# A two-layer decoder trunk on one core: the residual gates summed and spread by one product with ones, their bias by a transfer, and the adaLN vectors in another order

## The reference, cut to what matters

```python
c_act = jax.nn.silu(c)
for l in range(DEPTH):
    mod = (c_act @ w_ada[l] + b_ada[l])[:, None, :]
    sh1, sc1, gt1, sh2, sc2, gt2 = jnp.split(mod, 6, axis=-1)
    h = x * (1.0 + sc1) + sh1
    y = hybrid_mixer(h, positions, w_in[l], ...)      # window attention and top-k attention
    x = layer_norm(ALPHA * x + (1.0 + gt1) * y, ...)
    h = x * (1.0 + sc2) + sh2
    y = swiglu(h, w_gate[l], w_up[l], w_down[l])      # 1024 -> 2816 -> 1024
    x = layer_norm(ALPHA * x + (1.0 + gt2) * y, ...)
```

## Time and profile before

| | before |
|---|---|
| median of three runs | 1346.01 us |
| the profiled execution's own time | 1347.72 us |
| its span, first to last instruction | 1346.0 us |
| granted TensorE clock, mean | 0.982 |
| TensorE busy | 1266.8 us, 94% |
| VectorE, ScalarE, GpSimd busy | 61%, 37%, 21% |

### The profile page before, as it was taken

How to read it: one execution, slowest core, us unless ns; L and a number is a source line. 1 busy time by engine, 2 the same in 40 slices (tenths; PEclk the granted TensorE clock), 3 DMA queues, 4 the chain that set the end, 5 groups by cost and what they waited for, 6 DMA issues and landing times.

```text
span 1346.0 us, 18459 instructions
## 1 busy us (share of the span) xinstructions
PE 1266.8 (94%) x6392; PEld 1048.8 (78%) x6392; DVE 818.3 (61%) x1444; ACT 503.8 (37%) x1013; POOL 276.7 (21%) x287
## 2 busy tenths in 40 slices
PE   2798998999999999999999999899999999999996
PEld 2585876788888877888878888778888887888885
DVE  6667899757777756433266678975743355333337
ACT  0444657615333311232225455673443331222320
POOL 1084135811111100000002546563000000000001
PEclk9798999999899999999999999999999999999998
DMA  9553112242888725222222320011332223233311
GB/s 330 202 192 124 63 48 63 84 152 65 279 272 273 257 103 188 94 93 93 78 78 94 95 78 17 1 64 44 102 106 93 93 93 125 94 95 100 101 47 63
DMA packets 44272, 156.17 MB, mean 116 GB/s; under 512 B 5808, under 2 KB 5808, under 8 KB 44208
## 3 DMA queue, kind: packets, MB, share of 16 engines
q1 hardware_dynamic: 30528, 109.07, 24.2%
q0 software_dynamic: 12672, 46.14, 10.3%
q10 hardware_dynamic: 1008, 0.12, 0.1%
HBM read 153.21 MB, written 2.10 MB: 115 GB/s over the span
## 4 chain that ended last, share of the span: by engine, by line
PE 73%; DVE 13%; issue 4%; ACT 3%; POOL 3%; DMA 3%; SPq 0%; DVEq 0%; ACTq 0%; POOLq 0%
PE bank L539 22%; PE bank L541 21%; PE bank L540 21%; PE bank L805 2%; PE bank L772 2%; DMA ada_w<-in_w_ada 2%; DVE scores L1438 2%; DVE w_lo L1310 2%; DVE top L1430 2%; PE bank L751 2%; DVE ada_acc L1333 1%; DMA w_raw<-in_weights 1%; PE bank L783 1%; DVE xs L1540 1%; DVE pq L1477 1%
## 5 line engine op out<-in xcount | busy, mean ns | idle before, releaser
L539 PE MATMUL bank<-hT_hi,w_hi 128*128 128x512 f32 (+1 forms) x768 | 287.2, 374 | 2.2 <-issue 1.5
L540 PE MATMUL bank<-hT_lo,w_hi 128*128 128x512 f32 (+1 forms) x768 | 285.8, 372 | 0.0
L541 PE MATMUL bank<-hT_hi,w_lo 128*128 128x512 f32 (+1 forms) x768 | 285.7, 372 | 0.0
L1696 DVE TENSOR_TENSOR w_lo<-w_raw,w_hi 128x1024 fp32r<-128x1024 f32 x88 | 107.8, 1225 | 146.3 <-ACT w_hi L1220 146.3
L539 PE MATMUL bank<-w_hi,hT_hi 128*128 128x512 f32 (+2 forms) x448 | 172.1, 384 | 10.8 <-DVE hT_lo L1395 7.1
L1064 ACT ACTIVATE w_hi<-w_raw 128x1024 fp32r<-128x1024 f32 x96 | 100.5, 1061 | 211.5 <-PE bank L541 208.4
L539 PEld LDWEIGHTS bank<-hT_hi,w_hi 128*128 128x128 f32 x768 | 145.1, 189 | 28.1 <-issue 2.2
L541 PE MATMUL bank<-w_hi,hT_lo 128*128 128x512 f32 (+2 forms) x448 | 165.5, 369 | 0.0
L540 PE MATMUL bank<-w_lo,hT_hi 128*128 128x512 f32 (+2 forms) x448 | 165.3, 369 | 0.0
L541 PEld LDWEIGHTS bank<-hT_hi,w_lo 128*128 128x128 f32 x768 | 145.0, 189 | 25.3
L540 PEld LDWEIGHTS bank<-hT_lo,w_hi 128*128 128x128 f32 x768 | 145.1, 189 | 25.1
(11 more groups left out here) (144 smaller groups left out, 1894.9 us busy)
## 6 DMA issues: line engine op xcount, KB each, us to landing
w_raw<-in_weights SPq DMA_DIRECT2D x184, 512.0 KB, 3.4
ada_w<-in_w_ada POOLq DMA_DIRECT2D x80, 512.0 KB, 5.1
ada_w<-in_w_ada SPq DMA_DIRECT2D x16, 512.0 KB, 5.1
xs<-in_x SPq DMA_DIRECT2D x4, 512.0 KB, 9.2
g_row<-in_ln_row POOLq DMA_DIRECT2D x4, 512.0 KB, 5.6
b_row<-in_ln_row POOLq DMA_DIRECT2D x4, 512.0 KB, 6.3
trunk_out<-xs SPq DMA_DIRECT2D x8, 256.0 KB, 2.0
modb<-in_b_ada ACTq DMA_DIRECT2D x1, 48.0 KB, 3.7
```

Of the source, the lines that this page charges most:

```text
L539: pe.matmul(dst, a_hi, b_hi, start=first, stop=False)
L540: pe.matmul(dst, a_hi, b_lo, start=False, stop=False)
L541: return pe.matmul(dst, a_lo, b_hi, start=False, stop=last)
L1696: nc.vector.tensor_tensor(w_lo[:, s, :], w_raw[:, s, :], w_hi[:, s, :].bitcast(F32), ALU.subtract).then_inc(lo_ready, 1)
```

## The change: what it does

The vectors are made in the order sh1, sc1, sh2, sc2, gt1 of layer 0, then sh1, sc1, sh2, sc2 of layer 1, then gt2 of layer 0, gt1 and gt2 of layer 1. The first four, and the four of layer 1, remain in column form; they are the only ones that are reduced. A gate's accumulator is instead multiplied by a 128 by 128 matrix of ones, which sums over the partitions and puts the sum on all of them. Its bias comes as a row to `scratch` by a broadcast transfer (GpSimd issues that of the first gate at step 33 of attention, ScalarE that of the second behind group 0's `feed`), and `take_gate` computes (sum + 1) + bias.

The accumulations keep their places up to vector 4. Turn 0 of the loop has none; turns 1 to 4 have vectors 5 to 8, turn 5 vector 9. Vector 10 is accumulated after DN00's residuals, and vector 11 after DN01's. The wait for the taken vectors moves from DN00's first tile to its last. `reduce_ada` writes to bank 3 and not to bank 0. In `build_h` the wait for `gt_spread` becomes one for `gt_taken`.

```diff
-SH1, SC1, GT1, SH2, SC2, GT2 = range(6)
+SH1, SC1, SH2, SC2, GT1, GT2 = range(6)
+ADA_ORDER = ((0, SH1), (0, SC1), (0, SH2), (0, SC2), (0, GT1), (1, SH1), (1, SC1), (1, SH2), (1, SC2),
+             (0, GT2), (1, GT1), (1, GT2))
+ADA_COLUMNS = 8
...
+        def acc_of(g):
+
+            return g % 2 if g < 5 else int(g not in (9, 11))
...
+                    if i == ROPE_AT[-1]:
+                        pool.wait_ge(roped, at_roped(l, 4, T - 1))
+                        pool.dma_start(scratch[:], b_gate[2 * l].to_broadcast([P, D_MODEL])).then_inc(gate_in[0], 16)
...
             def spread_gate(l, which, b):
 
-                pe.wait_ge(gt_diag, 2 * l + which + 1)
+                g = ADA_ORDER.index((l, (GT1, GT2)[which]))
+                pe.wait_ge(ada_used, (g + 1) * KD)
                 for half in range(2):
-                    m = pe.matmul(bank[b + half][:], ones[:], scratch[:, half * 512:(half + 1) * 512],
+                    m = pe.matmul(bank[b + half][:], ones[:], ada_acc[:, acc_of(g), half * 512:(half + 1) * 512],
...
-                    if l == 0:
-                        reduce_ada(0)
                 else:
                     pe.wait_ge(z_done, at_z(l, DN00, T - 1))
-                with pe.Fori(1 - g, FG[g] // 2) as i:
-                    for j in range(4):
-                        wait_turn(j, i)
-                        product(j, slice(0, SEQ)).then_inc(piece_used, 1)
-                    if (l, g) == (0, 0):
-                        reduce_ada(i)
+                with_ada = (l, g) == (0, 0)
+                for i0, i1 in ((1, 5), (5, 6)) if with_ada else ((1 - g, FG[g] // 2),):
+                    with pe.Fori(i0, i1) as i:
+                        for j in range(4):
+                            wait_turn(j, i)
+                            product(j, slice(0, SEQ)).then_inc(piece_used, 1)
+                        if with_ada and i1 == 5:
+                            reduce_ada(i)
...
-                        pe.wait_ge(mod_taken, 5 + FG[0] // 2)
+                    elif q == DN00 and t == T - 1:
+
+                        pe.wait_ge(mod_taken, ADA_COLUMNS)
...
                 if l == 0:
-                    reduce_mod(3, 7, KD)
-                    reduce_mod(4, 7)
+                    reduce_mod(3, 7)
...
-                    if (l, g) == (0, 1):
-
-                        reduce_mod(6 * DEPTH - 1, 7)
...
+                act.wait_ge(h_lo, at_tile(2 * l + 1, T - 1))
+                act.wait_ge(h_hi, at_tile(2 * l + 1, T - 1))
+                act.dma_start(scratch[:], b_gate[2 * l + 1].to_broadcast([P, D_MODEL])).then_inc(gate_in[1], 16)
...
             def take_gate(l, which, b):
+
+                dve.wait_ge(gate_in[which], 16 * (l + 1))
                 dve.wait_ge(gt_spread, 2 * l + which + 1)
                 for half in range(2):
-                    m = nc.vector.tensor_copy(gt_row[:, half * 512:(half + 1) * 512], bank[b + half][:])
+                    cols = slice(half * HALF, (half + 1) * HALF)
+                    m = nc.vector.scalar_tensor_tensor(out=gt_row[:, cols], in0=bank[b + half][:], scalar=1.0,
+                                                       in1=scratch[:, cols], op0=ALU.add, op1=ALU.add)
...
-                    if i == GATE_AT:
-                        gate_diagonal(l, 0)
...
+                for i0, i1 in ((0, 1), (1, 5), (5, 6)) if with_ada else ((0, FG[g] // 2),):
+                    with dve.Fori(i0, i1) as i:
+                        for f in range(2):
+                            if with_ada and i0 > 0:
+                                ada_pieces(i, ada_acc[:, acc_of(4 + i0), :], 4 * f, 4 * f + 4)
...
-                gate_diagonal(l, 1)
...
                     for t in range(T):
                         residual(l, q, t, True)
-                    if (l, half) == (0, 0):
-                        ada_group(6 * DEPTH - 1)
+                    if l == 0:
+                        ada_group(10 + half)
```

More of the change, by code:

```diff
@@ L557, in transpose_x, with reduce_mod @@
                 m.then_inc(x_transposed, 1)
[L559 removed]
+            def reduce_mod(g, b):
                 if g == 0:
@@ L564, in reduce_mod @@
                 for k in range(KD):
-                    m = pe.matmul(bank[b][:, c0 + k:c0 + k + 1], ada_acc[:, g % 2, k * P:(k + 1) * P], ones[:, 0:1],
+                    m = pe.matmul(bank[b][:, k:k + 1], ada_acc[:, g % 2, k * P:(k + 1) * P], ones[:, 0:1],
                                   start=True, stop=True)
@@ L1325, in ada_piece, with take_mod @@
                     dve.wait_ge(ada_in[n % RING], 16 * ((n - 2 * KD) // RING + 1))
+                acc = ada_acc[:, acc_of(g), :]
                 if k == 0:
[L1327 to L1331, removed]
-                else:
[L1333 to L1337, removed]
+                    if g == 11:
+                        dve.wait_ge(gt_spread, 2)
+                    elif g >= 2:
+                        dve.wait_ge(mod_reduced, min(g - 1, ADA_COLUMNS))
+                    nc.vector.tensor_scalar(acc, ada_w[:, n % RING, :], cc[:, 1, 0:1], None, ALU.mult)\
+                        .then_inc(ada_used, 1)
+                else:
+                    nc.vector.scalar_tensor_tensor(out=acc, in0=ada_w[:, n % RING, :], scalar=cc[:, 1, k:k + 1],
+                                                   in1=acc, op0=ALU.mult, op1=ALU.add).then_inc(ada_used, 1)
+            def take_mod(g, b):
                 dve.wait_ge(mod_reduced, g + 1)
-                nc.vector.tensor_tensor(mod[:, g, :], bank[b][:, c0:c0 + KD], modb[:, g, :], ALU.add)\
+                nc.vector.tensor_tensor(mod[:, g, :], bank[b][:, 0:KD], modb[:, g, :], ALU.add)\
                     .then_inc(mod_taken, 1)
@@ L1707, in ada_pieces @@
                         else:
                             dve.wait_ge(ada_used, i * KD + n)
[L1709 to L1711 removed]
+                            m = nc.vector.scalar_tensor_tensor(out=acc, in0=ada_w[:, n % RING, :],
+                                                               scalar=cc[:, 1, k:k + 1], in1=acc,
+                                                               op0=ALU.mult, op1=ALU.add)
@@ L1712, in ada_pieces @@
                         m.then_inc(ada_used, 1)
[L1714 to L1727, removed]
-                                                gu_hi[:, at, :].bitcast(F32), ALU.subtract).then_inc(gu_lo_ready, 1)
-                        dve.wait_ge(gu_lo_ready, i * 2 + (f0 + f + 1))
-                    if with_ada:
-                        dve.wait_ge(mod_reduced, i + 6)
-                        nc.vector.tensor_tensor(mod[:, bass.ds(i + 5, 1), :],
-                                                bank[0][:, 0:KD].unsqueeze(1),
-                                                modb[:, bass.ds(i + 5, 1), :], ALU.add).then_inc(mod_taken, 1)
@@ L1890 @@
     one, zero = np.ones((D_MODEL,), np.float32), np.zeros((D_MODEL,), np.float32)
+    b_vectors = b_ada.reshape(DEPTH, 6, D_MODEL)
+    order = [6 * l + (0, 1, 3, 4, 2, 5)[v] for l, v in ADA_ORDER]
     rows = np.stack([np.stack([g, b]) for l in range(DEPTH)
```

67 lines of the change are left out of this document (34 added, 33 removed).

## The result

| | before | after |
|---|---|---|
| median | 1345.87 us (6 runs, 1343.45 to 1348.15) | 1337.07 us (6 runs, 1334.94 to 1339.17) |
| ratio, 95% interval | | 0.9936 [0.9923, 0.9949] |
| profiled execution, its span | 1347.72, 1346.0 us | 1335.96, 1334.2 us |
| granted TensorE clock, mean | 0.982 | 0.989 |

The kernel became 8.8 us faster, with an interval that excludes 1; 6.3 were forecast, and the new median lies within the stated range. The page of the kernel after, engine totals and chain by engine, beside the earlier trace rows: 64 matmuls less, and TensorE's share of the chain stays the largest.

What follows compares the result with a forecast made beforehand. TensorE, busy 94% of the span, was taken as the bound. Removed work and waits of 16.5 us, less 3.4 for the spread and 6.8 for vector 11, gave -6.3: median 1346.0 to 1339.7 us, range 1334.0 to 1343.5.

Steps and rivals of the forecast that it cites:

- Reductions at 1.7 us each: Four of twelve reductions on TensorE go; those between WO0 and WO1 and ahead of DN10 save 1.7 us each.
- Turn 0, -7.8: End of group 0's turn 0: a 2.71 us wait, a 1.7 reduction and 3.4 of lower clock go, 7.8 us.
- Turn 5 to DN00, -5.3: Between turn 5 and DN00: reduction and wait of 3.7 us and 1.65 of lower clock go, 5.3 us.
- The spread, +3.4: Ahead of layer 0's first gate spread: TensorE waits 1.8 us, the clock falls for 1.65; cost 3.4 us.
- Vector 11, +6.8: Group 1's third product waits 5.1 us behind vector 11, plus 1.7 for a clock fall; cost 6.8 us.
- DN01, nothing: The stretch of DN01 in layer 0 was forecast to change by 0 us.
- (a): Rival, chance 0.14: group 1's stall only 1.7 us without a fall, none in attention; -13.0 us, 1333.
- Diagonals, takings, transfers, sums: nothing: Four diagonals and takings removed from VectorE count nothing; added bias-row transfers and sums cost nothing to under 0.1 us each.
- (b): Rival, chance 0.10: turn 1 finds low halves or raw pieces late, turn 0 gives only 1.7; -0.2 us, 1345.8.
- (c): Rival, chance 0.08: vector 11's first four pieces not loaded at 545.9, stall 12.5 us, fall 3.4; +2.8 us, 1348.8.

Runs made afterwards that it cites:

- e6_reduce5: The kernel after with one reduction more at the end of turn 5, its vector waited for at DN00's last tile: 1337.23 us, ratio 0.9938.
- e2_turn0: Against `e3_gate0`, layer 1's four columns come first, in turns 0 to 3, and are reduced there; gates follow in turns 4 and 5: 1335.59 us, ratio 0.9922.
- e3_gate0: The kernel after with layer 0's second gate as vector 5, summed in turn 0 and not reduced; nothing in DN01: 1329.87 us, ratio 0.9878.
- e4_late_spread: The kernel after with the spread of each layer's first gate behind WO0's first tile, not ahead of it: 1334.34 us, ratio 0.9910.
- e7_reduce5_wait: As `e6_reduce5`, but with the wait for the taken vector at DN00's first tile, as in the kernel before: 1341.99 us, ratio 0.9963.
- e1_swap: The kernel after with the low halves of group 1's third and fourth piece ahead of vector 11 in VectorE's queue: 1329.87 us, ratio 0.9877.
- after_again: The kernel after measured once more, with no edit: 1338.2 us, ratio 0.9933 to the kernel before.

## Why the prediction was right, term by term

- *Reductions at 1.7 us each.* Right. Measured 1.8 between WO0 and WO1, 1.8 ahead of DN10, 1.8 in `e6_reduce5`. The earlier trace rows gave it.
- *Turn 0, -7.8.* Right: -7.9, and 7.96 the other way in `e2_turn0`. That it is a wait for a result and no lack of room on VectorE was read from the earlier trace rows and argued from 5.8 us of slack in the earlier trace rows; `e3_gate0` showed it.
- *Turn 5 to DN00, -5.3.* Right, in its parts too: 1.8, 1.6 and 1.6 in the two kernels that put them back.
- *The spread, +3.4.* Here a term was mis-sized: +1.4 was measured. The idle time is 1.41, not 1.8: the last piece took 1.28 us and not the 1.66 of the earlier trace rows, as VectorE's timeline of the kernel after has it:

```profile
265.28 0.69 DVE L1530 TENSOR_TENSOR hT_lo<-bank,hT_hi 128x512 fp32r<-128x512 f32 x1
265.88 1.28 DVE L1346 SCALAR_TENSOR_TENSOR ada_acc<-ada_w,cc,ada_acc 128x1024 f32<-128x1024 f32 x1
```

And the clock did not fall behind it, in none of the seven profiles (of six kernels) that have the wait. I had taken the fall on the strength of the earlier trace rows, where waits of 1.52 and 1.85 bring it and one of 1.80 does not; between such rows it was a guess. The same trace has another wait of 1.80 us, up to 218.86, with 0.50 behind it, which I had not read (more in the last section). The sum came out within 2.5 us of the measured time in spite of this term, not by it. The term is 2.0 of the 2.6 us by which the sum fell short of the -8.9 of the trace.
- *Vector 11, +6.8.* Right: +7.1. Order 2.1 (1.7 forecast), waits for `ada_w` 3.3 in this profile (3.4 forecast from the earlier trace rows; 1.7 to 2.9 in the other four), fall of the clock 1.7. In `e4_late_spread` and `e7_reduce5_wait` the clock stayed at 0.50 for 6.8 us there, the upper bound of the forecast. `e1_swap` removed the whole by an exchange of two blocks.
- *DN01, nothing.* 0.5 us more was gained. One of its pieces had been waiting for a low half behind old vector 11, 0.25 us of idle time in the record and a start 0.4 late, and does so no more:

```profile
527.20 0.47 PE L539 MATMUL bank<-w_hi,gu_hi 128*128 128x512 f32 x1 [0.25 <-DVE w_lo L1310]
```

VectorE's waits for `ada_w` in this place went from 3.4 to 2.5 us. The likely cause is that the two rows of the norm, whose transfers ran there in the kernel before, now come later; no run tests it. I had named it under rival (a), without a number.
- *Diagonals, takings, transfers, sums: nothing.* Right. Layer 1, which has two gates and no other edit, has the same shift at every mark from its second half of attention to the end, but for one residual on VectorE that is off by 0.3 us and delays nothing.
- *The rivals.* (a) asked for a stall of 1.7 without a fall in group 1, and that did not come (5.3 and 4.3 us, each with a fall); what is true of it is that the wait in attention brings no fall. (b) and (c) did not come: turn 1's pieces were in time, and vector 11's first four pieces were loaded.

What the Trainium skill says of transfers issued by GpSimd beside VectorE ("SBUF — State Buffer", Who interferes with whom) was taken in the forecast to ask for up to 5 us of such delay at vector 11. That read the rule too widely. By the same section of the Trainium skill an instruction of VectorE with two inputs in SBUF, as seven of vector 11's eight pieces are, contends only with what GpSimd reads, and the section infers that writing descriptors needs the write side. No excess over the earlier trace rows was seen, which agrees: the waits for `ada_w` sum to 3.3 and 2.2 us in the two profiles of the kernel after, 3.4 before. But no run here separates descriptor writing from plain traffic in those waits; that stays open.

## What to carry to other kernels

When work is moved between engines' queues, price it by who waits for its result, not by how busy the engine is: the same eight accumulations in turn 0 cost nothing when nobody waits for their sum, and 6.1 us when TensorE reduces it at once, beside the reduction itself. Ask what stands behind a moved block in its own queue and when that is wanted; if the next item is wanted sooner than the block is long, exchange the two. And carry a wait of the bounding engine at its price with the slower clock behind it, but as two terms: in the first profile the two waits came within 0.4 us of the forecast, of the two falls only one came.

## What the runs showed of the hardware that was not expected

A wait of about the same length was followed by a stretch at 0.50 in one execution and not in the next. The wait of 1.52 us at about 190 us is in all ten profiles of this study; behind it the clock fell in three (the kernel before, `after_again`, `e1_swap`). The timeline row and the stretch in the kernel after, and then the same two in `after_again`:

```profile
190.02 0.48 PE L783 MATMUL bank<-kT,qT 128*128 128x256 f32 x1 [1.52 <-DVE nmax L1480]
```
```profile
190.20:193.60 3.40, 3.15 (x17) 2.42 (x18) 3.37 (x11) 3.29 (x11) 2.42 (x3) 1.00 0.00 0
```
```profile
191.77 0.79 PE L783 MATMUL bank<-kT,qT 128*128 128x256 f32 x1 [1.52 <-DVE nmax L1480]
```
```profile
191.90:195.10 3.20, 3.20 (x9) 2.52 (x10) 3.17 (x10) 3.09 (x11) 2.17 (x3) 0.50 0.00 0
```

The wait of 1.41 us ahead of the spread had none behind it in seven. Nor does the length of the wait decide: one instruction waits 1.80 us in either layer of the kernel after, with the clock at 0.50 from within that wait on in layer 0 and at 1.00 in layer 1.

```profile
217.38 0.45 PE L794 MATMUL bank<-ident,pq 128*128 128x128 f32 x1 [1.80 <-DVE pT L1490]
859.57 0.30 PE L794 MATMUL bank<-ident,pq 128*128 128x128 f32 x1 [1.80 <-DVE pT L1490]
```
```profile
216.90:220.20 3.30, 2.82 (x10) 2.47 (x11) 2.96 (x14) 2.96 (x12) 2.82 (x3) 0.50 0.04 12
...
859.60:864.00 4.40, 4.08 (x27) 3.23 (x28) 4.37 (x17) 3.52 (x12) 3.81 (x3) 1.00 0.01 2
```

The first is so in all seven profiles with 1.80 us at that place (in the other three the clock falls 1 to 3 us before the wait there, which is shorter), the second in all ten. The kernel before even has a fall at 812 us with no wait over 0.6 us in the 10 us ahead of it. What brings a fall stays open.

What one costs depends on the place. Where TensorE is busy throughout, 3.4 us at 0.50 cost 1.6 to 1.7 (DN00, group 1). In attention, where it waits for others anyway, the one at 191 us cost the kernel before 0.8, and the one at 812 us 1.4, by the marks given under the table. So profiles of one kernel differ without any cause in the kernel. The two of the kernel after have spans of 1334.2 and 1336.1 us: 1.8 of the difference stand at 121 us, in the start; 0.7 and 0.5 come with lower clocks in attention, and 0.9 go back in group 1. Marks on both sides of an edit tell 2 us apart where medians with such differences in them cannot.

A sum over partitions cost TensorE no less here for having few columns. The eight products with a single column of ones kept it for 459.24 - 457.54 = 1.70 us in `e6_reduce5`; the spread of a gate, which sums the same 1024 columns and writes the sum to all 128 partitions, for 272.50 - 271.19 = 1.31 us in `e4_late_spread`.
